# Gating product of every up block on GpSimd instead of VectorE, issued behind the block's accumulating transfer

## What is computed

```
def conv_ffn(h, w_up, conv_w, conv_b, w_down):
    u = h @ w_up                                   # 256 x 2048 @ 2048 x 11264
    u = lax.conv_general_dilated(u, ...) + conv_b  # causal, depthwise, width 3
    gate, val = jnp.split(u, 2, axis=-1)
    return (jax.nn.silu(gate) * val) @ w_down      # 256 x 5632 @ 5632 x 2048
```

## Time and profile before

| | |
|---|---|
| median of 3 runs | 2496.64 us (2495.29 to 2497.62) |
| span of the profiled execution | 2494.1 us, core 0, granted clock 1.000 |
| PE busy | 2487.8 us, 100% |
| DVE busy | 2100.0 us, 84% |
| ACT busy | 1464.0 us, 59% |
| POOL busy | 44.3 us, 2% |
| the ring's loads (queue q1) | 56.5% of the 16 engines' span |

### The profile page before, as it was taken

The page is one execution under the profiler, slowest core; times in us unless marked ns, Lnnn a source line. Parts: engine busy times, 40 slices in busy tenths (PEclk is TensorE's granted clock), DMA queues, the critical chain, the costliest instruction groups (busy, mean ns, idle before and its releaser), DMA issues.

```text
span 2494.1 us, 30623 instructions
## 1 busy us (share of the span) xinstructions
PE 2487.8 (100%) x11823; PEld 2088.7 (84%) x11823; DVE 2100.0 (84%) x2387; ACT 1464.0 (59%) x1561; POOL 44.3 (2%) x54
## 2 busy tenths in 40 slices
PE   9999999999999999999999999999999999999999
PEld 8988888888888888888888888888888888888887
DVE  6656666999999999998778878776699999999998
ACT  5545555766767566556545545545566676766654
POOL 1000000000000000000000000000000000000000
PEclk9999999999999999999999999999999999999999
DMA  8554554757667557476556666654476666755754
GB/s 283 180 164 162 177 198 139 247 192 248 207 214 225 193 187 244 169 227 196 157 161 188 188 190 195 185 164 152 149 251 204 220 221 206 234 186 200 240 174 159
DMA packets 364820, 491.16 MB, mean 197 GB/s; under 512 B 19285, under 2 KB 216101, under 8 KB 362256
## 3 DMA queue, kind: packets, MB, share of 16 engines
q1 hardware_dynamic: 360448, 465.64, 56.5%
q0 software_dynamic: 4000, 23.63, 4.3%
q10 hardware_dynamic: 240, 0.10, 0.0%
HBM read 468.31 MB, written 3.68 MB: 189 GB/s over the span
## 4 chain that ended last, share of the span: by engine, by line
PE 98%; DVE 1%; ACT 0%; DMA 0%; issue 0%; ACTq 0%
PE psum L1945 43%; PE psum L1949 22%; PE psum L1831 8%; PE psum L1832 8%; PE psum L1838 8%; PE psum L2048 2%; PE psum L1958 1%; PE psum L1957 1%; PE psum L1956 1%; PE psum L2175 1%; PE psum L1787 0%; PE psum L2139 0%; PE psum L2173 0%; PE psum L2147 0%; PE psum L2159 0%; DVE w_lo L1116 0%
## 5 line engine op out<-in xcount | busy, mean ns | idle before, releaser
L1945 PE MATMUL psum<-w_hi,xT 128*128 128x512 f32 x3936 | 984.7, 390 | 0.0
L666 ACT ACTIVATE w_hi<-w_raw 128x2048 fp32r<-128x2048 f32 (+1 forms) x350 | 631.5, 1810 | 397.3 <-PE psum L1949 262.8
L1945 PEld LDWEIGHTS psum<-w_hi,xT 128*128 128x128 f32 x3936 | 736.6, 188 | 151.8
L1116 DVE TENSOR_TENSOR w_lo<-w_raw,w_hi 128x2048 fp32r<-128x2048 f32 (+1 forms) x332 | 705.3, 2145 | 55.7 <-ACT w_hi L666 55.4
L1949 PE MATMUL psum<-w_lo,xT 128*128 128x512 f32 x1968 | 516.0, 389 | 0.1
L1949 PEld LDWEIGHTS psum<-w_lo,xT 128*128 128x128 f32 x1968 | 369.3, 188 | 77.5 <-DVE w_lo L1116 1.0
L1831 PE MATMUL psum<-w_hi,xT 128*128 128x512 f32 (+1 forms) x1008 | 362.0, 369 | 0.0
L1832 PE MATMUL psum<-w_hi,xT 128*128 128x512 f32 (+1 forms) x1008 | 355.9, 363 | 0.0
L1124 DVE TENSOR_TENSOR w_lo<-w_raw,w_hi 128x2048 fp32r<-128x2048 f32 (+1 forms) x118 | 255.7, 2179 | 41.0 <-ACT w_hi L679 40.6
L679 ACT ACTIVATE w_hi<-w_raw 128x2048 fp32r<-128x2048 f32 (+1 forms) x118 | 215.3, 1830 | 102.7 <-PE psum L1949 63.1
L1945 PE MATMUL psum<-w_hi,mixT 128*128 128x512 f32 x896 | 239.6, 389 | 0.0
(11 more groups left out here) (201 smaller groups left out, 1919.1 us busy)
## 6 DMA issues: line engine op xcount, KB each, us to landing
w_raw<-in_f_w_up SPq DMA_DIRECT2D x352, 512.0 KB, 5.1
w_raw<-in_f_w_down SPq DMA_DIRECT2D x176, 512.0 KB, 5.1
w_raw<-in_b_w_qkv SPq DMA_DIRECT2D x192, 256.0 KB, 3.9
w_raw<-in_a_w_qkv SPq DMA_DIRECT2D x94, 512.0 KB, 4.4
w_raw<-in_b_w_qkv SPq DMA_DIRECT2D x256, 128.0 KB, 2.6
w_lo<-w_raw POOLq DMA_DIRECT2D x18, 1024.0 KB, 7.0
w_raw<-in_a_w_o SPq DMA_DIRECT2D x16, 1024.0 KB, 5.1
w_raw<-in_b_w_qkv SPq DMA_DIRECT2D x32, 512.0 KB, 6.2
```

Source lines behind the costliest of these rows:

```text
L666: nc.scalar.activation(w_hi[:, slot, cols], w_raw[:, slot, cols], ACT.Copy).then_inc(hi_ready, 1)
L1116: nc.vector.tensor_tensor(w_lo[:, slot, cols], w_raw[:, slot, cols], w_hi[:, slot, cols], ALU.subtract).then_inc(lo_ready, 1)
L1945: pe.matmul(o, x[:, h, P * m:P * (m + 1)], hi, start=start and h == 0, stop=False)
```

## The change

`gated` leaves DVE's program and stands in POOL's. POOL's order in an up stage is, for each block t: the accumulating transfer of block t's e2 (if it has one), then the product of block t-1; and behind the last block the product of block 10. The product waits for `val_taps` and `silu_ready` as before and raises `h_ready` as before.

```diff
-            def add_lows(layer):
-                for n, c in enumerate(DMA_LOWS):
-                    if UP0[layer] <= c < DN0[layer] + DOWN:
-                        pool.wait_ge(lo_negated, n + 1)
-                        pool.dma_start(w_lo[:, c % SLOTS, :], w_raw[:, c % SLOTS, :],
-                                       accum_op=ALU.add).then_inc(lo_added[n % 2], 16)
+            def gated(t, tg):
+
+                pool.wait_ge(val_taps, tg + 1)
+                pool.wait_ge(silu_ready, tg + 1)
+                h = hT[:, bass.ds(t * 4, 4), :]
+                nc.gpsimd.tensor_tensor(h, c_gate, h, ALU.mult).then_inc(h_ready, 1)
+
+            def up_stage(layer):
+                for t in range(UP_BLOCKS):
+                    first = UP0[layer] + UP_FIRST[t]
+                    for n, c in enumerate(DMA_LOWS):
+                        if first <= c < first + len(UP_ENTRIES[t]):
+                            pool.wait_ge(lo_negated, n + 1)
+                            pool.dma_start(w_lo[:, c % SLOTS, :], w_raw[:, c % SLOTS, :],
+                                           accum_op=ALU.add).then_inc(lo_added[n % 2], 16)
+                    if t > 0:
+                        gated(t - 1, UP_BLOCKS * layer + t - 1)
+                gated(UP_BLOCKS - 1, UP_BLOCKS * (layer + 1) - 1)
...
-            add_lows(0)
+            up_stage(0)
...
-            add_lows(1)
+            up_stage(1)
...
-            def gated(t, tg):
-
-                dve.wait_ge(val_taps, tg + 1)
-                dve.wait_ge(silu_ready, tg + 1)
-                h = hT[:, bass.ds(t * 4, 4), :]
-                nc.vector.tensor_tensor(h, c_gate, h, ALU.mult).then_inc(h_ready, 1)
-
...
                     split_up(c + 5)
-                    gated(t - 1, tg - 1)
...
                     split_up(c + 4)
-                    gated(t - 1, tg - 1)
...
                 taps(layer, 0, 1, UP_BLOCKS - 1, last)
-                gated(UP_BLOCKS - 1, last)
```

## The result

The changed kernel takes 2510.56 us (median of 4, 2506.14 to 2513.12), the kernel before 2495.97 beside it: ratio 1.0057, 95% interval 1.0043 to 1.0072. It is slower by 14.6 us. The profiled execution has a span of 2504.4 us against 2494.1, so 10.3 us of the loss can be read in its trace. Lines of the changed kernel are shifted: L1428 is now L623 on POOL, L1116 is L1128, L1142/L1145/L1147 are L1154/L1157/L1159, L666 is L678, L668 is L680, L866 is L878, L2048 is L2050.

What follows compares the result with a forecast made beforehand. PE's own work was taken to bound the kernel; with or without a full stop on DVE, PE loses 0 us, so span 2494.1 + 0 and median 2.5 us above it: 2496.6 us, range 2494 to 2501.

Steps and rivals of the forecast that it cites:

- e2: Chunk in an up block that ACT rounds and negates; ACT's rounding at 533.50 was given over 20 us of slack.
- What bounds the kernel before: Up blocks: PE's own work, 43.15 of 43.28 us; at most some 2.9 us to win off PE in all.
- Added on POOL: 22 products of 128x1024 on POOL, 2.45 us each, scaled by length from an add of 1.836 us.
- The stop: DVE's two-input operations beside POOL's product: taken as a full stop of 2.45 us, net 1.31 us per block.
- e7: Second `sum` chunk in up blocks: slack before PE falls from 2.13 to 0.82 us, tightest block 1.74 to 0.43.
- It is given back within the block: DVE idles 2.16 us per up block; busy 42.45 stays under 43.30 us, so the delay does not pile up.
- The sign of being wrong: PE idle before L1949 at e7 with DVE as releaser in each of 18 blocks, or a growing block period.
- Who waits: ACT has over 20 us of slack, POOL's queue holds nothing up, late loads reach e0 with 7.8 us: no cost.
- e0: Next block's chunk, first behind the late loads: low part wanted by PE at 539.23, 7.8 us of slack less 1.31.
- e4: Chunk in an up block that ACT rounds and DVE then subtracts; the prediction gave no figure for it.
- The forecast: Whole kernel: span 2494.1 + 0, median 2496.6 us, range 2494 to 2501, chance of same 0.90.
- Rival 1: At e7, a hold over 3.27 us exceeds the slack: slower, 2501 at 3.4 us, 2526 at 4.9; chance 0.10.

Runs made afterwards that it cites:

- late_b10dve: Changed kernel with the products of blocks 0 to 9 on POOL waiting also for p1_out, block 10's product left on DVE: 2496.12 us, ratio 1.0000.
- dose_big: Kernel before, product on DVE, plus two extra DVE operations (about 1.9 us in all) ahead of each of 22 products: 2529.49 us, ratio 1.0132.
- The dose: Kernel before, product on DVE, plus one extra DVE operation of about 0.94 us ahead of each of 22 products: 2511.1 us, ratio 1.0053.
- only_b10: Kernel before with only the product of block 10 (2 of 22, start of the down stage) moved to POOL: 2497.74 us, ratio 1.0006.

## Why the prediction was wrong

- **What bounds the kernel before.** Right, and with it the ceiling of a gain: late_b10dve takes 20 x 1.14 us off DVE and nothing comes off the time.
- **Removed from DVE, 1.14 us each.** Right.
- **Added on POOL, 2.45 us.** The product takes 2.24 to 2.28 once it has the port. The listed 3.29 to 4.39 contain its wait for it.
- **The stop.** Right in kind and place, and a little too large: 2.08 instead of 2.45, net 0.94 instead of 1.31. Here the rule of the Trainium skill, page "SBUF — State Buffer", section "Who interferes with whom", is borne out: the two-input operations are stopped in full (2.77 for 0.69 us), those with one input from PSUM are not (0.69 beside the product).
- **e7.** Its slack fell from 2.13 to 1.15 in the first block, 0.54 and 0.24 in the next two, and stayed there in layer 0; in layer 1 it lay between 0.23 and 0.79. PE never waited for it, as forecast.
- **"It is given back within the block."** This is the step that failed. I added up DVE's idle time (2.16 us) and took it for slack. It isn't: the 0.68 us ahead of the subtraction at 529.10 in rows 4 are a wait for ACT, which waits for a load, which waits for DVE's own subtraction of e7. When e7 is later, all of them are, and the idle time stays as long (0.86 us at the same place in the changed kernel). The whole way around, 42.8 us on average against 43.26, had about 0.4 us to spare, and the net delay was 0.94. The sign of being wrong that I had named, a growing period, is what came.
- **Who waits.** I followed the late loads to the chunk they bring and found 7.8 us of slack for e0. I didn't follow them to what stands behind their rounding on ACT, in its fixed order: the scaling that PE's transposes wait for, and the rounding of e4 that DVE waits for. At the transposes the margin was 1.0 to 2.5 us in the blocks before.
- **The forecast** of 2496.6, 2494 to 2501, with 0.90 for no change, was outside by 10 us. **Rival 1** had the sign, with 0.10, but the wrong condition: it wanted a hold over 3.27 us at e7. The hold was 2.24, and it was enough elsewhere. Its gate exists, as dose_big shows, but it opens second.

The profiled execution lost 10.3 us, the median 14.6. The dose and the change both spread over 7 to 8 us from run to run, against 2.5 to 5 for the kernel before. The loads' time to land is part of the loop, and it varies: from e7's end to the start of e2's rounding it is 11.1 us at 533.50 in the kernel before and 12.1 at 623.50 in the changed one, with the same issue times behind e7. The change did not make them slower: the average is 11.9 in the kernel before and 11.8 in the changed one. But within the changed one it is 12.0 in layer 0, whose blocks lost 4.19 us, and 11.6 in layer 1, whose blocks lost 1.73. That the variation makes the difference between profile and median was not tested.

## What to carry to other kernels

Idle time on an engine is slack only if what ends it doesn't hang on that engine's own earlier work. Where buffers are reused in a ring, follow a delay all the way around, through the slot, the load and everything queued behind the load's first reader, and compare the length of that loop with the period; a slack taken at one point of it says nothing of the others. A cheap way to ask the chip is a dose: add a known delay at the place in question to the kernel as it is, before the change is built. And when work goes to POOL, put it beside DVE operations that have an operand in PSUM.

## What the runs showed of the hardware that was not expected

A product on POOL that finds a two-input DVE operation running waits for its end and then goes ahead of DVE's next one, in all 22 cases in the changed kernel, so a busy DVE doesn't keep POOL out. It needs no gap for that: between L1154 and L1157 there are 0.03 us (599.23, 599.26), but in only_b10 the next operation is listed from 900.85, 0.08 us before the running one ends, and is stopped all the same. The listed duration of a POOL instruction includes that wait: 3.29, 3.94 and 4.38 us for the same 2.24 to 2.28 of work.
